# Three rounds of up and down chunks in the expert stage of a hybrid decoder

## The reference

```
# per token x; 8 heads, 128 x 128 = 16384 experts
q = x @ w_q;  s1, s2 = q1 @ k1.T, q2 @ k2.T        # per head, 128 + 128 scores
top 16 of s1, top 16 of s2, top 16 of their 256 sums -> ids, scores
g = softmax(scores)
act = u[ids] . x                                    # 16 dot products a head
w = g * gelu(act)
y = sum over heads and top 16 of w * v[ids]
```

## Time and profile before

| what | value |
|---|---|
| median of 3 runs | 3246.19 us (3244.92 to 3250.03) |
| profiled execution | 3250.2 us from first to last instruction |
| TensorE busy | 3225.4 us |
| VectorE busy | 2563.3 us |
| ScalarE busy | 1519.1 us |
| moved by DMA | 894.78 MB |
| activation stores and loads | 120 and 120, of 352 KB |

### The profile page before, as it was taken

The page is one execution under the profiler, slowest core; times in us unless marked ns, Lnnn a source line. Parts: engine busy times, 40 slices in busy tenths (PEclk is TensorE's granted clock), DMA queues, the critical chain, the costliest instruction groups (busy, mean ns, idle before and its releaser), DMA issues. The chain is left out here.

```text
span 3250.2 us, 55293 instructions
## 1 busy us (share of the span) xinstructions
PE 3225.4 (99%) x19718; PEld 3038.7 (93%) x19718; DVE 2563.3 (79%) x4920; ACT 1519.1 (47%) x2310; POOL 1101.5 (34%) x713
## 2 busy tenths in 40 slices
PE   8999999999999999999999999999999999999998
PEld 8878888999999999999988788889999999999998
DVE  6654349999997899999866543599999878999998
ACT  5553233477773333333355533334777733333333
POOL 1000014334345555555300000242343366555552
PEclk9999999999999999999999999999999999999999
DMA  4214322589999999999721143235999999999996
GB/s 148 77 53 143 142 94 87 192 321 381 381 379 409 412 400 409 404 407 411 285 91 66 66 146 140 85 113 181 356 380 379 379 404 419 401 402 406 401 405 255
DMA packets 230931, 894.78 MB, mean 275 GB/s; under 512 B 22784, under 2 KB 67984, under 8 KB 182912
## 3 DMA queue, kind: packets, MB, share of 16 engines
q1 hardware_dynamic: 116944, 465.34, 37.7%
q0 software_dynamic: 93008, 337.91, 26.6%
q10 hardware_dynamic: 20832, 89.74, 6.8%
HBM read 801.42 MB, written 91.49 MB: 275 GB/s over the span
## 5 line engine op out<-in xcount | busy, mean ns | idle before, releaser
L1402 PE MATMUL bank<-xT_hi,hi 128*128 128x352 f32 (+1 forms) x2688 | 926.6, 345 | 1.9 <-DVE xT_lo L951 1.7
L901 DVE TENSOR_TENSOR lo<-raw,hi 128x2048 fp32r<-128x2048 f32 (+2 forms) x320 | 699.9, 2187 | 278.6 <-ACT hi L552 269.6
L1404 PE MATMUL bank<-xT_hi,lo 128*128 128x352 f32 (+1 forms) x2688 | 910.6, 339 | 0.0
L1403 PE MATMUL bank<-xT_lo,hi 128*128 128x352 f32 (+1 forms) x2688 | 910.5, 339 | 0.0
L552 ACT ACTIVATE hi<-raw 128x2048 fp32r<-128x2048 f32 (+2 forms) x338 | 620.4, 1835 | 373.6 <-PE bank L1404 333.0
L1404 PE MATMUL bank<-w_hi,lo 128*128 128x352 f32 x2048 | 662.4, 323 | 0.0
L1402 PE MATMUL bank<-w_hi,hi 128*128 128x352 f32 x2048 | 661.2, 323 | 0.7 <-DVE w_lo L1320 0.6
L1403 PE MATMUL bank<-w_lo,hi 128*128 128x352 f32 x2048 | 658.1, 321 | 0.0
L541 POOL DMA_INDIRECT rows<-in_v_rows,ids x256 | 417.4, 1630 | 350.8 <-DVE h L1292 276.3
L1402 PEld LDWEIGHTS bank<-xT_hi,hi 128*128 128x128 f32 x2688 | 506.0, 188 | 31.9 <-issue 5.7
L1404 PEld LDWEIGHTS bank<-xT_hi,lo 128*128 128x128 f32 x2688 | 505.4, 188 | 25.4
(11 more groups left out here) (232 smaller groups left out, 4192.3 us busy)
## 6 DMA issues: line engine op xcount, KB each, us to landing
raw<-in_stream SPq DMA_DIRECT2D x352, 1024.0 KB
gate_d<-gate_s ACTq DMA_DIRECT2D x22, 2048.0 KB
act_d<-act_s ACTq DMA_DIRECT2D x120, 352.0 KB
act_in<-act_d SPq DMA_DIRECT2D x120, 352.0 KB
gate_in<-gate_d SPq DMA_DIRECT2D x96, 384.0 KB
gate_in<-gate_d SPq DMA_DIRECT2D x32, 256.0 KB
rows<-in_u_rows,ids POOLq DMA_INDIRECT x256
rows<-in_v_rows,ids POOLq DMA_INDIRECT x256
```

The source lines that it names most:

```text
L901: dve.tensor_tensor(lo[s][:, 0:n], raw[s][:, 0:n], hi[s][:, 0:n].bitcast(F32), ALU.subtract).then_inc(lo_done, 1)
L1402: pe.matmul(dst, a_[0], b_[0], start=first, stop=False)
L1403: pe.matmul(dst, a_[0], b_[1], start=False, stop=False)
L1404: return pe.matmul(dst, a_[1], b_[0], start=False, stop=last)
```

## The change

The last 18 up chunks are no longer followed by all the down chunks. They come in three rounds (`ROUNDS`, `SPAN`): six up chunks, then the six down chunks that use the same experts. Then the other 46 down chunks follow as before. So steps 0 to 45 are up, 46 to 51 up, 52 to 57 down, 58 to 63 up, 64 to 69 down, 70 to 75 up, 76 to 81 down, 82 to 127 down. The array `stream` is laid out in that order.

The activations of the 18 stay on chip, in `act_k`, `act_s` and `act_in`; 46 are stored in place of 60. Up chunks need banks 0 and 1, so after each round DVE copies or adds these two into `y_sum` (`round_sums`), and at the layer's end adds them to the last part. In the last down chunk of a round the two are computed first (`CLOSING`). The gate table is stored so that the rotated order of the experts begins with the last 36 of 128 rows, in two DMAs per slice, and its first four loads move to the steps of the table `GATES_AT`. Row operations are spread over steps 44 to 125 in shares of 16 for an up step and 13 for a down step (`rows_by`). TensorE's program has two up chunks and the first round written out, then a loop of two passes over a whole round, then the loop over pairs of down chunks; ACT's steps 44 to 81 are written out.

```diff
-KEPT = V_CHUNKS
-ACT_PAIRS = (C_U - KEPT) // 2
+ROUNDS, SPAN = 3, 6
+KEPT = ROUNDS * SPAN
+SPILLED = C_U - KEPT
+ACT_PAIRS = SPILLED // 2
+KEPT_ROWS = 2 * KEPT
+SHARED = 2
+BY_ACT, BY_DVE = (0, 2, 4, 5), (1, 3, 6, 7)
+GATES_AT = {50: (0, 0), 51: (0, 2), 52: (1, 0), 53: (1, 1), 54: (1, 2), 55: (1, 3),
+            62: (2, 0), 63: (2, 1), 64: (2, 2), 65: (2, 3), 70: (3, 0), 71: (3, 1), 72: (3, 2), 73: (3, 3),
+            74: (4, 0), 75: (4, 1), 76: (4, 2), 77: (4, 3)}
+UP_SHARE, DOWN_SHARE, ROWS_END = 16, 13, 2 * C_U - 2
+def rows_by(q):
+    if q < FIND_STEPS + G_STEPS:
+        return (q - FIND_STEPS) * ROWS_IN_G // (G_STEPS - 1)
+    shares = [UP_SHARE if x in UP_OF else DOWN_SHARE for x in range(FIND_STEPS + G_STEPS, ROWS_END)]
+    return ROWS_IN_G + sum(shares[:q + 1 - FIND_STEPS - G_STEPS]) * (ROW_OPS - ROWS_IN_G) // sum(shares)
...
-                    act.dma_start(gate_d[w], gate_s[:, w % 2].rearrange("p i t -> p (i t)")).then_inc(gate_out[w % 2], 16)
+                    first = P - KEPT_ROWS
+                    for i, to in (slice(0, first), slice(KEPT_ROWS, P)), (slice(first, P), slice(0, KEPT_ROWS)):
+                        act.dma_start(gate_d[w, :, to.start * SLICE:to.stop * SLICE],
+                                      gate_s[:, w % 2, i].rearrange("p i t -> p (i t)")).then_inc(gate_out[w % 2], 16)
...
+                        elif r > 0:
+                            act.wait_ge(w_done, l * C_V + (r - 1) * SPAN + x + 1 + CR)
...
+                def round_sums(r):
+                    for d in range(SHARED):
+                        dve.wait_ge(round_ps, SHARED * (ROUNDS * l + r) + d + 1)
+                        if r == 0:
+                            last = dve.tensor_copy(y_sum[:, d], ps[d][:, 0:TU])
+                        else:
+                            last = dve.tensor_tensor(y_sum[:, d], y_sum[:, d], ps[d][:, 0:TU], ALU.add)
+                        last.then_inc(round_ev, 1)
...
+                for q in range(FIND_STEPS + G_STEPS, 2 * C_U - 1):
+                    ahead(lp + P_U + q // 2, q % 2)
+                    c = DOWN_OF.get(q, -1)
+                    if c < KEPT and c % SPAN == SPAN - 1 and c >= 0:
+                        round_sums(c // SPAN)
+                    if q == WEIGH_ROWS_AT:
                         weigh_rows()
+                    if q + 1 in DOWN_OF:
+                        weigh_step(DOWN_OF[q + 1])
+                        if n < rows_by(q):
+                            row_op(n)
+                            n += 1
+                        weigh_lo(DOWN_OF[q + 1])
+                    while n < rows_by(q):
                         row_op(n)
                         n += 1
...
+                def round_of(r):
+                    up, down = ACT_PAIRS + SPAN // 2 * r, SPAN // 2 * r
+                    place = ACT_PAIRS + SPAN * r
+                    first = isinstance(r, int) and r == 0
+                    for x in range(SPAN):
+                        for i in range(2):
+                            if x == 0 and not first:
+                                pe.wait_ge(round_ev, SHARED * (ROUNDS * l + r) - 1 + i)
+                            experts(up + x // 2, x % 2, i, place=place + x // 2)
...
+                    for x in range(SPAN):
+                        s = x % 2
+                        take(lp + P_U + place + SPAN // 2 + x // 2, s)
+                        pe.wait_ge(w_done, l * C_V + 2 * down + x + 1 + CR)
+                        if x == 0:
+                            last = weighted(s, opens=range(NK) if first else range(SHARED), bank_free=turned_out)
+                        elif x == SPAN - 1:
+                            last = weighted(s, CLOSING, closes=range(SHARED), closed=round_ps)
+                        else:
+                            last = weighted(s)
+                        last.then_inc(w_used, 1)
+                round_of(0)
+                with pe.Fori(1, ROUNDS) as r:
+                    round_of(r)
```

More of the change, by code:

```diff
@@ L415, in acts_of @@
         def acts_of(k, s):
[L417 removed]
+            return (act_k, act_s, act_in)[k % SPAN // 2][:, s] if isinstance(k, int) and k < KEPT else act_in[:, s]
         @block.sync
@@ L878, in v_steps @@
                             weights_hi(2 * j + s + 1, 1 - s)
-                for j in range(ROW_PAIR):
-                    v_steps(j)
-                act.wait_ge(row_done, ROW_OPS * l + U_ROW_OPS)
-                act.activation(w_row[:], act_row[:], ACT.Gelu).then_inc(row_gelu, 1)
-                with act.Fori(ROW_PAIR, C_V // 2 - 1) as j:
+                with act.Fori(KEPT // 2, C_V // 2 - 1) as j:
                     v_steps(j)
@@ L889, in _ @@
                 squares(2 * l + 2, 0, 1)
-                for x in range(0, NK, 2):
+                for x in BY_ACT:
                     act.wait_ge(v_ps, NK * l + x + 1)
@@ L1675, in _, with experts @@
                 q_steps(PH // 2 - 1, True)
-                def experts(j, s, i, first=0, end=NK, halved=None):
+                def experts(j, s, i, first=0, end=NK, halved=None, place=None):
                     k = l * C_U + 2 * j + s
@@ L1731, in _, with weighted @@
                     g_step(st)
-                with pe.Fori(J_TAIL, C_U // 2) as j:
-                    for s in range(2):
-                        for i in range(2):
-                            experts(j, s, i)
-                pe.wait_ge(g_ev, GROUPS * (l + 1) + G_RING)
-                def weighted(s, first=False, last=False):
+                for c in range(FIND_STEPS + G_STEPS, SPILLED):
+                    for i in range(2):
+                        experts(c // 2, c % 2, i)
+                def weighted(s, order=V_BLOCKS, opens=(), closes=(), bank_free=None, closed=None):
@@ L1740, in weighted @@
                     v = chunk(s, P, 2 * NK)
-                    for x, d in enumerate(V_BLOCKS):
-                        if first and x >= NK - 2:
-                            pe.wait_ge((gelu0, gelu1)[d], C_U * (l + 1) + 1)
+                    for d in order:
+                        if bank_free is not None and d < SHARED:
+                            bank_free(d)
                         for i in range(2):
                             done = product(ps[d][:, 0:TU], at(v, i * NK + d), at((w_hi, w_lo), s, i),
-                                           first and i == 0, last and i == 1)
-                        if last:
-                            done.then_inc(v_ps, 1)
@@ L1754, in v_steps @@
                         pe.wait_ge(w_done, l * C_V + 2 * j + s + 1 + CR)
-                        weighted(s, first and s == 0).then_inc(w_used, 1)
-                v_steps(0, True)
-                with pe.Fori(1, C_V // 2 - 1) as j:
+                        if first and s == 0:
+                            last = weighted(s, opens=range(SHARED), bank_free=summed)
+                        else:
+                            last = weighted(s)
+                        last.then_inc(w_used, 1)
+                v_steps(KEPT // 2, True)
+                with pe.Fori(KEPT // 2 + 1, C_V // 2 - 1) as j:
                     v_steps(j)
```

184 lines of the change are left out of this document (95 added, 89 removed).

## The result

The changed kernel takes 3257.24 us (median of 8 runs, 3252.5 to 3259.38) against 3246.85 us (8 runs, 3243.67 to 3250.03) of the kernel before: a ratio of 1.0028, 95% interval 1.0019 to 1.0037. By the ratio it is slower by 9 us, with an interval of 6 to 12. In a second set of runs (experiment 5) the ratio was 1.0024 (1.0015 to 1.0034). Forecast were +2.5 us and "within 0.2%". The profiled execution has a span of 3257.3 us, 7.1 us over that of before; each is one execution of several, and that of before was one of the long ones of its kernel.

A forecast was written before the change was run, and what follows sets the result against it. TensorE's matmuls were taken to bound the kernel. Passages (1.3 us) and sums (0.75 us) a layer gave 4.1 us, less 1.6 us lost before: +2.5 us, 3248.7 us on the median; range 3243 to 3254.5 us.

The forecast's parts named there:

- part 5, gates: Gate loads beside weight loads at steps 50 and 51: excess transfers hidden, cost 0, at most 1.3 us a layer.
- a wait on a weight load near steps 50 to 53: Around the first down chunks of round one: one of the listed signs that the prediction was wrong.
- are full, but they bound nothing: Kernel before: transfers run at 397 to 420 GB/s, yet the only wait on a weight transfer is ScalarE's 2.0 us.
- Part 3, passages: Three passages from up to down chunks in each layer, not one: 1.3 us a layer, bounds 0.24 and 2.2.
- Part 4, the sums: Shared sums at round ends: 0 behind rounds one and two, 0.75 us a layer behind round three, bounds 0.4 and 1.1.
- Parts 1, 2 and 6: Fourteen more activations kept on chip, 0; chunk order, 0; block 0 moved to VectorE at layer end, 0 within 0.1 us.
- the jump: Round loop's jump over 1152 instructions: short, 0.21 us, costing nothing; rival long jump, 1.0 us a layer, chance 0.2.
- The sum: Both layers: 4.1 us of new gaps, less 1.6 us lost before, so +2.5 us.
- The rival of the pace: Down chunks: added stalls drop both layers from 7.68 to 7.73 us a chunk, 6.4 us more, 3255.1 us; chance 0.14.

The follow-up runs named there:

- experiment 5: The changed kernel run again without any edit, on another chip and for a second trace; ratio 1.0024 to the kernel before.
- kernel 2: Changed kernel with the shared sums of round three placed behind the making of `w_lo` and not ahead of it; ratio 1.0015 to the kernel before.
- kernel 1: Changed kernel with the first eight gate parts one to a step (steps 48 to 55), not four in steps 50 and 51; ratio 1.0005 to the kernel before.
- kernel 8: Changed kernel with only the row operations moved, as in kernel 6; gate parts and sums stay as in the change; ratio 0.9994 to the kernel before.
- kernel 3: Kernel before with four gate parts moved from steps 54 to 60 to the last two up steps, two to each weight load; ratio 1.0032 to the kernel before.
- kernel 4: Changed kernel with the edits of kernel 1 and kernel 2, and two row operations in each round's last up step; ratio 1.0014 to the kernel before.
- kernel 6: Changed kernel with the edits of kernel 1 and kernel 2, and row operations with their gathers levelled over the steps; ratio 0.9998 to the kernel before.
- kernel 7: Changed kernel with the edit of kernel 1 and each layer's 46 activation loads halved; ratio 1.0019 to the kernel before.
- kernel 9: Kernel before with two row operations in its last up step, not four, and `weigh_rows` moved behind `w_lo`; ratio 1.0001 to the kernel before.

## Why the prediction was wrong, by its own steps

**The step that failed is part 5, gates.** It found the excess right (456 GB/s wanted at steps 50 and 51 against 420 measured, 1.3 us of the transfers), and then called it hidden, because a load is issued 11 us ahead and 1 MB takes 2.5 us "alone". It is never alone. The load of 1016.16 took 12.6 us beside gates and gathers, so the cover of 11 us was used up before the excess came, and about the whole excess went to TensorE: 1.50 and 1.56 us in the first trace, 1.06 and 1.36 in the second, against 0 forecast and 1.3 as upper bound. That makes 2.4 to 3.1 us for the kernel. Kernel 2, with the same order there, lost 0.94 us in one layer and nothing in the other, so the cover is at its edge and not gone in every layer. The prediction had itself named a wait on a weight load near steps 50 to 53 among the signs of being wrong. Kernels 1 and 8 take the gap away in two different ways, kernel 3 brings such a gap about in the old order, kernel 4 brings it back with the gate parts apart and one gather earlier: gates, gathers and weights in these steps have to be added. How the transfers of the three queues delay one another was not measured.

The same error stood a second time, unseen: the transfers "are full, but they bound nothing" held for the kernel before and was taken over for a changed order. A late load at step 90, ten steps behind the restart of the activation loads at step 80, cost 1.47 us in one layer of the first trace and 0.59 us in one of the second. That it comes from crowding is supported by kernels 6, 7 and 8, which have none; the exact reason why it is step 90 stays open.

**Part 3, passages.** Round two: 0.56 and 0.08 us forecast, 0.58 and 0.10 measured. Rounds one and three: 0.1 and 0.4 us forecast for their second chunks, at most 0.1 measured; the operations behind the first `w_lo` fitted. Row operations as the cause are shown by kernels 4, 6, 8 and 9.

**Part 4, the sums.** 0.75 us a layer forecast behind round three, 0.54 and a restart of 0.10 measured; the pair took 0.86 and not 0.95 us. Nothing at the ends of rounds one and two, as said. What the prediction did not see is that the excess belongs to the step and not to the place in it (kernel 2).

**Parts 1, 2 and 6, and the jump.** No gain from 20 MB less. The copies at a layer's end cost what was said: TensorE's next work starts 0.72 us behind the last down matmul before and 0.71 after. Two terms beside them were put at nothing and were not. The jump over a layer was 0.6 us longer in this pair of traces. It scatters: 3.46 to 3.74 us in the three traces of the kernel before and its variants, 3.77 to 4.33 us in the eight of the changed kernel and its variants. And from the last down matmul to the end of the span it is 14.5 us in all of these eight, 13.8 us in all of the three; what takes the 0.65 us is not shown. The jump over 1152 instructions took 0.21 us. The rule of the two pages of 16 KiB in "Runtime: NRT & Kernel Launch", section "Instruction fetch mechanics", of the Trainium skill, by which it would have stalled, was not borne out; its other figure, 2048 instructions for TensorE, agrees.

**The sum.** Forecast 4.1 us of gaps in place of 1.6; measured 7.7 and 6.2 in place of 1.6. In the two profiled executions the stretch from the last gate matmul to the last down chunk grew by 4.56 us in the first layer (645.95 to 650.51) and by 1.04 us in the second (649.04 to 650.08), 5.6 us together. The gaps are 6.1 of them, and the pace of the matmuls gave back 0.5. With 0.6 us for the jump over the layer, 0.65 at the end and 0.2 ahead of the rounds that is the difference of the two spans, 7.0 to 7.1 us. So beside the term of part 5, 1.2 us of the layers' ends were missing from the sum. The ratios give more, 9 us (6 to 12) and 8 us (5 to 11); the profiled execution of before was a long one, with the slow pace in its second layer, and what the ratios have above the traces is not accounted for one by one.

**The rival of the pace** had the right side, slower, for the wrong reason, as far as is shown. Kernels 6 and 8 keep the rounds, the sums and all passages, lose the gaps, and lie at 0.9998 and 0.9994. The pace is real, but it scatters both ways (below): the profiled execution of kernel 6, at 3243.5 us, ran its last 46 chunks at the fast pace in both layers, that of kernel 8, at 3248.1 us, at the middle one. That the changed kernel's runs are not also slower in pace on average, because they stall more often, was not tested. The chance of 0.14 for "slower" rested on it alone; a rival "the transfers' backlog uses up the 11 us" was missing.

## What to carry to other kernels

Where transfers run at their limit, the cover of a load is its lead less the time that loads take *in that stage beside all others*, gathers of another engine included; here 11 us of lead held hardly any. A late load also delays the issue of a later one. A change that brings no more bytes can still put them into one step, and gate loads moved two by two next to weight loads cost more than 20 MB taken away gave. When an engine fills 7.0 of 7.7 us of the average step (VectorE, 91% in the stretch below), extra work has to be paid by taking something out of that step, not by moving it within it. The best version, kernel 8 or 6, is only as fast as the kernel before, since TensorE bounds it and its work did not change.

## What the runs showed of the hardware that I had not expected

**The pace of the same matmuls has three values.** In the long loop of down chunks the mean distance of matmuls stays the same for hundreds of microseconds, and it is 158.9, 160.0 or 161.1 ns, at a granted clock of 1.00. It can go from one to another at a stall, and also where up and down chunks meet with no distance above 0.33 us (kernel 6). One view of each value (windows as in the earlier trace rows; columns PE, PEld, DVE, ACT, POOL, clock, DMA share, GB/s), first the changed kernel, then kernel 6; two of the matmuls counted straddle the edges:

```profile
1340.00:1600.00 260.00, 260.00 (x1627) 260.00 (x1627) 237.30 (x190) 91.74 (x68) 139.13 (x86) 1.00 1.02 404
2900.00:3200.00 300.00, 300.00 (x1864) 300.00 (x1864) 273.13 (x218) 105.95 (x78) 164.85 (x101) 1.00 1.02 406
```

```profile
1230.00:1600.00 370.00, 370.00 (x2330) 370.00 (x2330) 337.79 (x271) 130.91 (x98) 193.39 (x119) 1.00 1.00 394
```

260 us by 1625 is 160.0 ns, 300 by 1862 is 161.1, 370 by 2328 is 158.9. Over the 46 chunks of the last loop the outer two differ by 4.9 us. Which one is left behind looks like chance. It may be a good part of why runs of one kernel spread over 6 us and more, which one profiled execution of each kernel can't show. Up chunks in the rounds had 160.0 or 161.1 ns; in the tail of the kernel before always 160.0.

**A stall of some us can cost more than itself.** Behind the idle time of 4.2 us in the first layer of kernel 3 the granted clock was 0.50, the lower of its two levels, for the next 5.3 us, and the matmuls came 294 ns apart. In kernel 4 a distance of 2.20 us at 2945.07 was followed, about 1 us later, by some 12 matmuls 293 ns apart, and this stretch (columns as above) has a mean clock of 0.64:

```profile
2947.30:2952.00 4.70, 4.70 (x20) 4.70 (x21) 1.99 (x2) 1.91 (x1) 2.87 (x2) 0.64 1.04 419
```

The sums of the gaps of both kernels hold these stretches too. Behind the distances of up to 2.05 us no such stretch was seen.
